# Six and ten ring slots in place of eight and eight, and scores given out at an earlier place, in a two-layer decoder trunk

## The reference

```python
q = (xb @ w_query).reshape(tb, PEER_HEADS, 2, PEER_KEY_DIM // 2)
s = jnp.einsum('thpd,pnd->thpn', q, sub_keys).astype(jnp.float32)
top_s, top_i = lax.top_k(s, k)
cand_s = top_s[:, :, 0, :, None] + top_s[:, :, 1, None, :]
cand_i = top_i[:, :, 0, :, None] * PEER_N_KEYS + top_i[:, :, 1, None, :]
best_s, best_j = lax.top_k(cand_s.reshape(tb, PEER_HEADS, k * k), k)
idx = jnp.take_along_axis(cand_i.reshape(tb, PEER_HEADS, k * k), best_j, axis=-1)
gate = jax.nn.softmax(best_s, axis=-1)
u = expert_u[idx]
act = jax.nn.gelu(jnp.einsum('thkd,td->thk', u, xb).astype(jnp.float32))
w = (gate * act).astype(xb.dtype)
return jnp.einsum('thk,thkd->td', w, expert_v[idx])
```

## Time and profile before

| | before |
|---|---|
| median of 3 runs | 2017.28 us (2014.41 to 2019.20) |
| profiled execution | 2011.19 us, span 2008.8 us |
| PE busy | 1557.9 us, 78% |
| DVE busy | 1094.4 us, 54% |
| POOL busy | 1046.2 us, 52% |
| ACT busy | 370.7 us, 18% |
| mean granted TensorE clock | 0.873 of full speed |
| gathers | 1056, 553.72 MB, 71.7% of 16 DMA engines' time |

### The profile page before, as it was taken

The page is one execution under the profiler, slowest core; times in us unless marked ns, Lnnn a source line. Parts: engine busy times, 40 slices in busy tenths (PEclk is TensorE's granted clock), DMA queues, the critical chain, the costliest instruction groups (busy, mean ns, idle before and its releaser), DMA issues.

```text
span 2008.8 us, 14530 instructions
## 1 busy us (share of the span) xinstructions
PE 1557.9 (78%) x4050; PEld 720.5 (36%) x4050; DVE 1094.4 (54%) x2706; ACT 370.7 (18%) x948; POOL 1046.2 (52%) x1110
## 2 busy tenths in 40 slices
PE   8999987588777775888777874697876966777777
PEld 3477634245222222333333521243333422222223
DVE  2433245665665655456566564656665657646641
ACT  1032112122211111232021211221110311202111
POOL 1110023656666665456355574656554666666663
PEclk9955688888999897989888897998887998999999
DMA  4211136979999997889889997999988898999996
GB/s 171 87 42 43 41 108 242 416 294 357 362 370 372 375 367 282 322 314 366 323 316 358 366 400 296 364 362 404 409 312 312 328 381 329 361 390 350 369 386 231
DMA packets 184127, 616.74 MB, mean 307 GB/s; under 512 B 19276, under 2 KB 20812, under 8 KB 184055
## 3 DMA queue, kind: packets, MB, share of 16 engines
q0 software_dynamic: 152064, 553.72, 71.7%
q1 hardware_dynamic: 31990, 62.17, 8.3%
HBM read 614.77 MB, written 1.05 MB: 307 GB/s over the span
## 4 chain that ended last, share of the span: by engine, by line
PE 42%; POOL 17%; DMA 14%; DVE 12%; issue 11%; another core or an unknown queue 2%; ACT 1%; DVEq 0%; SPq 0%; POOLq 0%
POOL arena L570 16%; PE bank L849 16%; DMA arena<-peer_v,idx 11%; PE bank L651 11%; DVE arena L1496 3%; DMA arena<-peer_u,idx 3%; PE bank L752 3%; PE bank L823 2%; PE bank L984 2%; PE bank L724 1%; PE bank L713 1%; PE bank L640 1%; DVE h L1503 1%; PE bank L676 1%
## 5 line engine op out<-in xcount | busy, mean ns | idle before, releaser
L849 PE MATMUL bank<-arena 128*128 128x512 f32 x1968 | 989.4, 642 | 290.9 <-DMA arena<-peer_v,idx 154.3
L1496 DVE CUSTOM_DVE_ANT_0 arena<-arena,bank 128x1024 f32<-128x1024 f32 x528 | 621.8, 1218 | 185.1 <-DMA arena<-peer_u,idx 129.5
L570 POOL DMA_INDIRECT arena<-peer_v,idx x528 | 513.0, 972 | 370.5 <-PE bank L849 191.5
L849 PEld LDWEIGHTS bank<-arena 128*128 128x128 f32 x1968 | 370.9, 201 | 867.0 <-issue 417.1
L570 POOL DMA_INDIRECT arena<-peer_u,idx x528 | 504.1, 955 | 340.4 <-issue 148.1
L651 PE MATMUL bank<-wring,hT 128*128 128x512 f32 (+5 forms) x604 | 263.2, 592 | 19.9 <-DVE gws L1567 19.5
L1135 ACT ACTIVATE arena<-con,wgt 128x128 f32<-128x128 f32 x492 | 154.9, 389 | 344.9 <-PE bank L849 129.2
L651 PEld LDWEIGHTS bank<-wring,hT 128*128 128x128 f32 (+1 forms) x604 | 110.4, 184 | 169.3 <-issue 164.9
L1503 DVE SCALAR_TENSOR_TENSOR h<-arena,wgt,h 128x1024 f32<-128x1024 f32 x36 | 46.3, 1285 | 164.4 <-DMA arena<-peer_v,idx 150.8
L1450 DVE MAX8 top<-bank 128x8 f32<-128x128 f32 x66 | 16.4, 290 | 120.6 <-issue 87.2
L1126 ACT ACTIVATE gl<-dots 128x16 f32<-128x16 f32 x33 | 7.1, 216 | 391.5 <-issue 300.2
(11 more groups left out here) (157 smaller groups left out, 1035.7 us busy)
## 6 DMA issues: line engine op xcount, KB each, us to landing
wring<-gla_w_in SPq DMA_DIRECT2D x12, 2048.0 KB
arena<-peer_u,idx POOLq DMA_INDIRECT x528
arena<-peer_v,idx POOLq DMA_INDIRECT x528
wring<-gla_w_out SPq DMA_DIRECT2D x4, 2048.0 KB
wring<-peer_w_query SPq DMA_DIRECT2D x4, 2048.0 KB
wring<-attn_w_in SPq DMA_DIRECT2D x2, 2048.0 KB
wring<-attn_w_out SPq DMA_DIRECT2D x2, 2048.0 KB
gws<-peer_w_query SPq DMA_DIRECT2D x2, 2048.0 KB, 10.2
```

The costliest lines, as they stand in the source:

```text
L570: nc.gpsimd.indirect_dma_start(out=ring[:, k % RING, :], out_offset=None, in_=table.rearrange("l e d -> (l e) d"), in_offset=bass.Indirect ...
L849: last = nc.tensor.matmul(yacc[:, 512 * i:512 * i + 512], wdiag[:, k, :], vrow[:, k % RING, 512 * i:512 * i + 512], start=first, stop=last ...
L1496: v.tensor_tensor_reduce(out=urow[:, k % RING, :], in0=urow[:, k % RING, :], in1=xnow, scale=1.0, scalar=0.0, op0=ALU.mult, op1=ALU.add, a ...
```

## The change

The rings become 6 slots for first rows and 10 for second rows, in the same arena, and both count slots and landings through all tiles. The scores of tile i+2 go from behind mix 11 to behind mix 3 of the turn, except in turns 15 and 23, where they stay. The roots go from behind the gathers of pick 13 to behind those of pick 11.

```diff
-RING = 8
+U_RING, V_RING = 6, 10
...
+        def wait_landed(eng, kind, g, k):
+            landed, ring = ((u_in, U_RING), (v_in, V_RING))[kind]
+            n = TOPK * g + k
+            eng.wait_ge(landed[n % ring], 16 * (n // ring + 1))
...
             def gather(kind, g, k):
                 layer = GATHERED[g][0]
+                n = TOPK * g + k
                 if kind == 0:
-                    at_least(pool, u_used, TOPK * g + k - RING + 1)
-                elif k >= RING:
-                    wait_second_used(pool, g, k - RING)
-                elif g:
-                    wait_second_used(pool, g - 1, k + RING)
+                    at_least(pool, u_used, n - U_RING + 1)
+                elif n >= V_RING:
+                    wait_second_used(pool, (n - V_RING) // TOPK, (n - V_RING) % TOPK)
...
             chosen(0)
-            for k in range(RING):
+            for k in range(U_RING):
                 gather(0, 0, k)
             root(small[:, 1:2], small[:, 4:5], 1)
-            for k in range(RING, TOPK):
+            for k in range(U_RING, TOPK):
                 gather(0, 0, k)
...
-                    if k == 13 and i in STAGES:
+                    if k == 11 and i in STAGES:
                         for t in STAGES[i][0]:
                             mixer_root(t, STAGES[i][1])
-                    if k == 13 and i in (2, 26):
+                    if k == 11 and i in (2, 26):
...
-                    if k == 11 and i + 2 < TILES:
+                    if k == (11 if i in (15, 23) else 3) and i + 2 < TILES:
                         scores(i + 2)
```

More of the change, by code:

```diff
@@ L358, in build @@
         den_ready = sem("den_ready")
-        u_in = [sem(f"u_in{i}") for i in range(RING)]
-        v_in = [sem(f"v_in{i}") for i in range(RING)]
+        u_in = [sem(f"u_in{i}") for i in range(U_RING)]
+        v_in = [sem(f"v_in{i}") for i in range(V_RING)]
         u_used = sem("u_used")
@@ L450, in wait_second_used, with u_slot, v_slot @@
                 eng.wait_ge(v_mixed, MIXED[g] + by_tensor(g).index(k) + 1)
-        def landings(g, k):
-            return 16 * (g * (TOPK // RING) + k // RING + 1)
+        def u_slot(g, k):
+            return (TOPK * g + k) % U_RING
+        def v_slot(g, k):
+            return (TOPK * g + k) % V_RING
+        def wait_landed(eng, kind, g, k):
+            landed, ring = ((u_in, U_RING), (v_in, V_RING))[kind]
+            n = TOPK * g + k
+            eng.wait_ge(landed[n % ring], 16 * (n // ring + 1))
         block = ctx.enter_context(nc.Block())
@@ L586, in _ @@
             chosen(0)
-            for k in range(RING):
+            for k in range(U_RING):
                 gather(0, 0, k)
             root(small[:, 1:2], small[:, 4:5], 1)
-            for k in range(RING, TOPK):
+            for k in range(U_RING, TOPK):
                 gather(0, 0, k)
-            for k in range(RING):
+            for k in range(8):
                 gather(1, 0, k)
@@ L596, in _ @@
                 gather(0, 1, k)
-                if k < RING:
-                    gather(1, 0, k + RING)
+                if k < 8:
+                    gather(1, 0, k + 8)
             for i in range(2, TILES + 1):
@@ L845, in mix @@
                         at_least(pe, y_added, (g + PH - 1) // PH)
-                    pe.wait_ge(v_in[k % RING], landings(g, k))
+                    wait_landed(pe, 1, g, k)
                     pe.wait_ge(diag_ready, MIXED[g] + mine.index(k) + 1)
@@ L849, in mix @@
                         last = nc.tensor.matmul(yacc[:, 512 * i:512 * i + 512], wdiag[:, k, :],
-                                                vrow[:, k % RING, 512 * i:512 * i + 512], start=first, stop=last_one)
+                                                vrow[:, v_slot(g, k), 512 * i:512 * i + 512], start=first, stop=last_one)
                     last.then_inc(v_mixed, 1)
@@ L1494, in dot @@
                         add_second(g - 1, k)
-                    dve.wait_ge(u_in[k % RING], landings(g, k))
-                    v.tensor_tensor_reduce(out=urow[:, k % RING, :], in0=urow[:, k % RING, :], in1=xnow, scale=1.0, scalar=0.0,
+                    wait_landed(dve, 0, g, k)
+                    v.tensor_tensor_reduce(out=urow[:, u_slot(g, k), :], in0=urow[:, u_slot(g, k), :], in1=xnow, scale=1.0, scalar=0.0,
                                            op0=ALU.mult, op1=ALU.add, accum_out=dots[:, g % 2, k:k + 1]).then_inc(u_used, 1)
@@ L1500, in add_second @@
                 b = GATHERED[g][1]
-                dve.wait_ge(v_in[k % RING], landings(g, k))
+                wait_landed(dve, 1, g, k)
                 at_least(dve, v_added, ADDED[g] + by_vector(g).index(k))
-                v.scalar_tensor_tensor(out=h[:, b, :], in0=vrow[:, k % RING, :], scalar=wgt[:, g % 2, k:k + 1], in1=h[:, b, :],
+                v.scalar_tensor_tensor(out=h[:, b, :], in0=vrow[:, v_slot(g, k), :], scalar=wgt[:, g % 2, k:k + 1], in1=h[:, b, :],
                                        op0=ALU.mult, op1=ALU.add).then_inc(v_added, 1)
```

15 lines of the change are left out of this document (8 added, 7 removed).

## The result

The changed kernel takes 2151.75 us (median of 4 runs, 2141.96 to 2156.99), the kernel before on the same chip 2018.24 us (4 runs). The ratio is 1.0649, 95% interval 1.0597 to 1.0701: 133 us slower where the forecast had 39. The profiled execution took 2141.96 us, 2140.1 of them in the span, so 131.3 us more span than before.

What follows compares the result with a forecast made beforehand. It took DMA as nearly full in plain turns and a loop of waits as deciding shared turns. Terms 56 + 5 - 8 - 12, less 2 for turn 14, gave +39 on 2017.3: about 2057 us (2035 to 2075; wider range 2006 to 2112).

Steps and rivals of the forecast that it cites:

- the shared loop: Shared turns, dot 6 to the next addition: six first-row slots delay second-row gathers, 38.6 us becoming 47.9, taken for all.
- the term of 56 in the sum: Shared turns 11, 12, 14 and 18 to 22: the longer loop adds 56 us together; bounds 0 and 112.
- I count nothing for these four: Shared turns 10, 13, 15 and 23: existing DVE waits, for weights or PE, cover the longer addition waits; 0 us.
- The plain turns: Dot 5 holding u11 costs 3.7 us in ten turns, seven save 3; taken as +5 us, bounds -50 and +60.
- Where they go, dot 5 is done at some 26 us into the turn: Plain turns: without DVE's waits for scores, dot 5 comes in time for u11; about seven turns save 3 us.
- Both limits at once: Rival: all 19 plain turns get the u wait, DVE's steps being slow anyway; 70 us, 2122 us; chance 0.22.
- Scores: Scores at mix 3 end DVE's waits for keys; in shared turns 10 and 18 this saves 8 us, turn 14 2.
- Roots: Roots behind pick 11 avoid POOL's wait at v(9, 8), in turns 2, 10, 18 and 26: -12 us, bounds 0 and -25.
- Second rows: Ten slots remove POOL's waits for PE, about once a plain turn; 5.0 us of slack, but u11's wait replaces it.
- No change: Rival: the additions' waits lie beside PE's work in all turns and plain turns stay; about 2015 us; chance 0.06.
- Short landings: Rival: rows land 2.1 us sooner once POOL pauses, taking 50 us off the sum; 2006 us; chance 0.03.
- Faster: Rival: PE's late signals limit and two more v slots remove them; plain turns 42 us, 1986 us total; chance 0.14.

Runs made afterwards that it cites:

- e1: The changed kernel (six and ten slots, roots at pick 11) but with scores left at mix 11: 2154.05 us, ratio 1.0675 to the kernel before.
- e2: The kernel before (eight and eight slots, roots at pick 13) with only the scores moved to mix 3: 2017.06 us, ratio 1.0014.
- e9: The changed kernel run again unaltered, in the third set, where signals are late: 2152.02 us, ratio 1.0676 to the kernel before.
- e16: The changed kernel with eight and eight slots, and dots 5 to 7 ahead of the choice of experts in plain turns: 2025.58 us, ratio 1.0053 to before.
- e3: The changed kernel with only eight slots for second rows, six for first rows: 2122.99 us, ratio 1.0535 to the kernel before.
- e5: The changed kernel with every gather bringing half a row from a slot's second use on, in the set without late signals: one execution, 1863.23 us.
- e8: The changed kernel with dots 5 to 7 ahead of the choice of experts in plain turns, set without late signals: 1979.66 us, ratio 1.0494 to before.
- e12: The changed kernel with half the bytes in every gather but the first of a slot, in the third set, where signals are late: one execution, 2057.87 us.
- e13: The changed kernel with a pause on GpSimd behind pick 6 of plain turns (six writes): 2126.76 us, ratio 1.0553 to the kernel before.
- e7: The changed kernel with second rows gathered two picks behind the first rows' place, not four, set without late signals: 1868.55 us, ratio 0.9894 to before.
- e6: The changed kernel with eight and eight slots and a one-element GpSimd write behind each gather from tile 2, set without late signals: 1888.00 us, ratio 1.0004.

## Why the forecast was wrong in size

**The direction and the shared loop** were right. All 12 additions ahead of dot 8 now wait, 5.3 to 7.7 us. In the eight turns of the sum the stretch from dot 6 to the next addition is 47.5, 48.3 and 48.4 us in turns 11, 18 and 20, for the 47.9 of the working. Turn 20, against the earlier trace rows: dot 6 is done at 1430.10.

```profile
1430.10 0.08 DVE L1505 DVE_READ_ACCUMULATOR2_ANT dots<- 128x1 f32 x1
```

```profile
1478.46 1.28 DVE L1512 SCALAR_TENSOR_TENSOR h<-arena,wgt,h 128x1024 f32<-128x1024 f32 x1 [11.46 <-DMA arena<-peer_v,idx]
```

In the turns 12, 14, 19, 21 and 22 it is 52.4 to 53.7 us. "I take 47.9 for all" was the mistake there. In 19 the landing ahead of dot 4 was slow before too (11.5 us from the start of the issue) and stayed so (12.5). In 12, 14, 21 and 22 it is mostly the row ahead of dot 12: it took 8.6 to 10.5 us where the working had 6.3, so its addition started 25.0 to 27.5 us behind dot 6 and not 22.8. Together the eight stretches grew by some 82 us. The turns themselves grew by 64, the term of 56 in the sum: turn 18, with its earlier root and scores, takes 58.5 us for 58.8.

**"I count nothing for these four"** failed in turns 15 and 23, which grew by 10.1 and 8.7 us; 10 and 13 grew by 3.3 and 0.3. I took the wait for the weights as cover. It went, or fell to half in turn 10, as the same line shows now:

```profile
841.61 0.23 DVE L1531 SCALAR_TENSOR_TENSOR wgt<-gate_e,z,gl 128x16 f32<-128x16 f32 x1 [6.47 <-ACT gl L1135]
...
1169.64 0.23 DVE L1531 SCALAR_TENSOR_TENSOR wgt<-gate_e,z,gl 128x16 f32<-128x16 f32 x1 [0.27 <-issue]
```

On DVE it did cover the additions: counted from u(15, 0), the weights of tile 15 come at 84.8 us, and at 90.5 before. But POOL's u(16, 0) waits for a dot ahead of them, dot 10, and came 10 us later. Turn 16 gave nothing of it back (52.8 us for 53.7), since u(16, 2) and u(16, 11) waited 5.7 and 8.0 us for dots. A wait covers what stands ahead of it only for those who wait behind it.

**The plain turns** were the main error: +5 in the sum, +57.8 us in 13 turns. The step that failed is "Where they go, dot 5 is done at some 26 us into the turn". DVE's wait for scores was gone, and dot 5 was done at 33.7 to 37.8 us into these turns. In turn 7 DVE lost 13 us to late signals; before it had lost 15 us there to the wait for scores, with no pause in the choice of experts. It is not only that one wait had hidden the other. In turn 7 of e1, whose scores come at the old place, DVE has no wait for scores either, and the late signals stand in the same three places:

```profile
635.77 1.22 DVE L1505 CUSTOM_DVE_ANT_0 arena<-arena,bank 128x1024 f32<-128x1024 f32 x1 [3.58 <-remote]
...
645.58 0.09 DVE L1447 MATCH_VALUE_LOAD pairs<-best,pairs 128x8 f32 x1 [5.95 <-remote]
...
649.78 0.43 DVE L1450 MAX8 best<-pairs 128x8 f32<-128x256 f32 x1 [3.31 <-remote]
```

In e2, with early scores and eight slots, the choice of experts in turn 9 runs without them, and dot 5 is done at 28.9 us, in five of the 13 turns at 27.5 to 29.7:

```profile
722.24 0.09 DVE L1447 MATCH_VALUE_LOAD pairs<-best,pairs 128x8 f32 x1
...
723.16 0.43 DVE L1450 MAX8 best<-pairs 128x8 f32<-128x256 f32 x1
```

Turn 30 had the pattern before too; with six slots it comes in nearly every plain turn. Waits of over 2 us on DVE that no landing ended (from 9.5 to 45 us into the turn) are 22 in the 13 plain turns before and 19 in e2, but 36 in the changed kernel, 34 in e1 and 35 in e9. Why six slots bring more of them is open. The rival "Both limits at once" had dot 5 late for a reason that is not the scores and priced it at 70 us; turn 30 in the earlier trace rows, dot 5 at 36 us with no wait for scores ahead of it, was its evidence, and I gave it 0.22.

**The sum.** The measured parts are 64 for the eight turns, 22 for the four, 58 for the plain ones, -6 for the rest, and -7 outside the turns, of which 6 are scatter: 131 us. The scores and the roots are inside these parts and cannot be added again.

**Scores**: -10 in the sum, and no gain in the whole time (e2; e1 against e9). One turn shows a gain: turn 14 takes 71.9 us in e1 and 65.2 to 65.5 in the changed kernel and e9. **Roots**: -12 in the sum. The four turns with a root are 11.8 us shorter in e16 than in e2, but only 1.8 shorter in the changed kernel than before (219.4 and 221.2), and no whole time shows the gain; it was not measured alone. **Second rows**: POOL's waits for PE went as forecast. But PE's wait ended 30.7 us into the turn, and the gather right behind it is u(g, 11), which now waits to 37 us, so nothing was left for two slots to save; e3 shows that they cost instead. It has 25 of the waits counted above, where e1 has 34; what makes them fewer is open.

**The other rivals**: the additions' waits were not beside PE's work, so "No change" falls. The rows ahead of dot 8 took 4.8 to 6.6 us from the start of the issue to the addition, those ahead of dots 4 and 12 5.5 to 12.5, where "Short landings" needed 4.2. The waits for PE went and the plain turns grew all the same, so "Faster" falls.

## What to carry to other kernels

A ring's depth is not a buffer size alone: in an interleaved queue it sets which release each transfer stands behind, and a transfer that another engine waits for must not stand behind a release that this engine gives just before. Shift the queue's order with the depth (here LEAD), and the same memory gives that part of the time back. When a wait goes, look for an instance of the pattern that had no such wait and read how late its end is; it shows the next limit.

## What the hardware showed that was not expected

In the first comparison and in three of the four sets of runs signals between instructions arrive late in most plain turns, even from DVE to itself. DVE then waits up to four times in a turn, mostly 2.5 to 6 us each; PE's scores came up to 17 us behind their row. The kernel before takes 2012 to 2018 us there. In one set, e5 to e8, no trace has a single such wait, and the same kernel takes 1887 us. The set without them and both later sets with them have the same chip number; if a number means one and the same chip, it is no fixed property of a chip. Halving the bytes (e12) left it as it was (36 waits), and so did a pause of 2.2 us in POOL's gathers (e13, 33 waits). It is not TensorE's clock: the granted share was 1.00 in the window in which DVE only waited, as in the window of e7. What makes it is open. It decides what a change costs: plain turns lost 58 us by six slots where it is, and the 13 plain turns of e7 take 3.5 us more than those of e6, where it is not.

A gather of 512 KB takes 6.1 us from the start of its issue to the addition that waits for it, with a row of gathers ahead of it that has no gap (v4, 918.82 to 924.95); with v12 it is 6.6 (893.20 to 899.83), and with the v8 row, which has only u12 ahead of it behind a pause of 7.8 us, 5.2 (879.02 to 884.24). With half the bytes (e12) most of these rows take 3.4 to 3.8 us.
